# Four quarter loads of the input rows: issued together, or each when the one ahead has landed

## The chip, the cores and the metric

The kernel runs on one core of one Trainium2 chip. The time is device microseconds of that core for one execution, from the runtime's start of the program to its end; the profile's span (first to last instruction) is a little shorter. The engines are TensorE (PE in the rows; PEld is its weight load), VectorE (DVE), ScalarE (ACT), GpSimd (POOL) and SyncE (SP). A q behind an engine's name marks its queue, that is, instructions that only issue transfers. All inputs and outputs are in HBM; transfers from any engine move on the core's 16 DMA engines.

## The reference

One decoder step over 264 tokens (256 prompt rows, 8 decode rows) of width 1024, depth 1, all in float32. Cut to what matters here:

```python
def layer(x, ...):                    # x: 264 rows of 1024
    xn = rmsnorm(x, norm1)            # x * rsqrt(mean(x*x) + 1e-5) * norm1
    m, conv_new, ret_new = mixer(xn, ...)   # proj = xn @ w_in (1024 x 11264), short conv, retention
    h = x + m
    return h + moe_ffn(rmsnorm(h, norm2), ...)   # top 4 of 32 experts, clamped SwiGLU, 1024 wide
```

The first thing computed is therefore the sum of squares of each input row, the gain norm1, and the product of the rows with the first columns of w_in. The expert weights, 402 MB, are the bulk of all bytes.

## The kernel before

Every engine has its own instruction stream, and semaphores connect them. The mixer comes first, in an order of PE work that `mixer_order` writes out; weights come in 60 chunks of 1024 KB (`w_mixer`), which SP loads into a ring of 12 slots, each slot again as soon as its chunk was read. Then come routing and the experts in 16 pairs (`w_pairs`), whose weights SP loads in transfers of 2048 and 4096 KB, also slot by slot.

**The start, around the change.** The input rows are loaded turned (features along partitions) as `x_turned`, into `x_raw`: 8 groups of 128 features (k = 0 to 7) by 264 rows. `RAW_PARTS = 4` loads of two groups each (a quarter, 264 KB, `RAW_KS = 2`) stand at the head of ACT's stream (L915 to L917) and count the semaphores `raw_in[0..3]`. SP at the same time issues `par` (L636, 84 KB, the gains), the first two chunks of weights as 8 loads of 256 KB, one for each k (`load_first`, L634), tables (L623) and then whole chunks (L643).

- ACT: a dummy Sqrt (L923, it brings the table load with it), then for each quarter a wait for `raw_in[part]` and a Square of it into `x_squares` (L926, L927). Then the Sqrt of the sums (L929).
- DVE: for each k, after the wait for the quarter, `x_gained[k] = x_raw[k] * norm1` (L1246). Behind all eight of these, in the order of the stream, the squares are added up in four steps: L1248, L1250, L1252 and L1254, the last of which counts `x_summed`. Later the reciprocal (L1256) and the scaled tables.
- PE: `WARMING = 9` products of ones by ones (L1746), which nobody reads, then `project_first` (L1726): for k = 0 to 7 it waits for the weights of k and for `x_gained[k]` and makes four products into four banks (L1736). A float32 product appears as two passes in the trace. Behind k = 4 (`SUMS_BEHIND`) stands one product with ones (L1742), which adds the squares over partitions; it waits for `x_summed`. PE's stream is in order, so k = 5, 6 and 7 stand behind that wait. Then the second projection (L1722) and so on.

```python
for k in range(KD):                                  # PE, project_first
    pe.wait_ge(first_w[k], 16)
    pe.wait_ge(xg_ready, k + 1)
    ...
    if k == SUMS_BEHIND:
        pe.wait_ge(x_summed, 1)
        fills(pe.matmul(fill(pe, "x_sums")[:, 0:T], ones[:, :], x_squares[:, 0, :], start=True, stop=True), "x_sums")
```

Of the kernel before, what the change touches and what calls it, by code (L numbers as in the profile page):

```python
# [75 lines left out]
RAW_PARTS = 4  # L76
SUMS_BEHIND = 4
RAW_KS = KD // RAW_PARTS
WARMING = 9
WHOLE_CHUNKS = PAIR_CHUNKS - 2  # L80
SCRATCH = 2048
ARENA = 21672
# [288 lines left out]
def build(nc, a, o):  # L371
# [4 lines left out]
    with ctx:  # L376
# [202 lines left out]
        def read(eng, name):  # L579
            bank, n = plan[name]  # L580
            eng.wait_ge(filled[bank], n)
            return psum[bank]
# [37 lines left out]
        def _(sp):  # L620
            def load_tables(n):
                c = slice(TABLE_PARTS[n], TABLE_PARTS[n + 1])
                sp.dma_start(cst[:, c], a["tables"][:, c]).then_inc(cst_in[n], 16)  # L623

            mixer = [last for *_, last in mixer_parts()]
            assert len(mixer) == MIXER_CHUNKS

# [284 lines left out]

        @block.scalar
        def _(ac):
            for part in range(RAW_PARTS):  # L915
                ks_in = slice(RAW_KS * part, RAW_KS * (part + 1))
                ac.dma_start(x_raw[:, ks_in, :], a["x_turned"][:, ks_in, :]).then_inc(raw_in[part], 16)  # L917
            for primed in (xg_lo,):
                ac.sem_inc(primed, PRIMED)
            ac.sem_inc(quarter_squared, SQUARES)  # L920
# [3 lines left out]
            for part in range(RAW_PARTS):  # L924
                ks_in = slice(RAW_KS * part, RAW_KS * (part + 1))
                ac.wait_ge(raw_in[part], 16)  # L926
                ac.activation(x_squares[:, ks_in, :], x_raw[:, ks_in, :], ACT.Square).then_inc(x_squared, 1)  # L927
            bank = read(ac, "x_sums")
            empties(ac.activation(rinv[:, :], bank[:, 0:T], ACT.Sqrt, scale=1.0 / D, bias=stat[:, 15:16]), "x_sums")  # L929
# [269 lines left out]
        def _(v):  # L1199
# [71 lines left out]
            def rotate(event):  # L1271

                _, (name, g), j = event
                dst, cs, sn = (qT, cos, sin) if name == "q" else (kT, cosk, sink)
                if g == 0:
                    cs, sn = cos_r, sin_r
                lo, hi = ("proj", (name, g), j - 1), event
                x1, x2 = read(v, lo)[:, 0:T], read(v, hi)[:, 0:T]

                def times(i, x, table):  # L1280
                    if (name, g) == ("k", 0):
                        return v.scalar_tensor_tensor(rot[:, i, :], x, DK ** -0.5, table, ALU.mult, ALU.mult)
                    return v.tensor_tensor(rot[:, i, :], x, table, ALU.mult)  # L1283

                own(times(0, x1, cs))
                own(times(1, x2, sn))
                empties(times(2, x1, sn), lo)
                empties(times(3, x2, cs), hi)
                settle()
                was_read(v, lo)  # L1290
                was_read(v, hi)
                v.tensor_tensor(dst[:, j - 1, :], rot[:, 0, :], rot[:, 1, :], ALU.subtract).then_inc(qk_ready, 1)
                v.tensor_tensor(dst[:, j, :], rot[:, 2, :], rot[:, 3, :], ALU.add).then_inc(qk_ready, 1)
                qk[0] += 2
                v.wait_ge(qk_ready, qk[0])
# [397 lines left out]
        def _(pe):  # L1693
# [19 lines left out]
            def project(event):  # L1713

                _, name, j = event
                rhs, groups = {"wa": (aT, 1), "wb": (rT, 2)}.get(name[0], (x_gained if name == ("k", 0) else xnT, 1))
                n = chunks_of(name, groups)
                bank = fill(pe, event)
                for k in range(KD * groups):
                    if j == 0 and k % 4 == 0:  # L1720
                        chunk_ready(n + k // 4)
                    ins = pe.matmul(bank[:, 0:T], weight(n + k // 4, k % 4)[:, 128 * j:128 * (j + 1)], rhs[:, k, :],  # L1722
                                    start=k == 0, stop=k == KD * groups - 1)
                fills(ins, event)
# [19 lines left out]
            pe.wait_ge(const_set, 2)  # L1744
            for _ in range(WARMING):
                pe.matmul(psum[SUM_BANK][:, 0:128], ones[:, :], ones[:, :], start=True, stop=True)  # L1746
# [485 lines left out]
```

## Time and profile before

| | |
|---|---|
| median of 3 runs | 1411.05 us (1409.99 to 1411.69) |
| profiled execution, its time | 1411.89 us |
| its span | 1410.1 us |
| mean granted TensorE clock | 0.991 |
| PE, DVE, ACT, POOL busy | 96%, 27%, 18%, 7% of the span |
| bytes moved | 519.97 MB, mean 369 GB/s |

The profiled execution's time is 1.8 us more than its span, the part before the first and behind the last instruction, and 0.84 us more than the median. Engines' busy shares are averages over the whole span; the views below are of stretches.

### The profile page before, as it was taken

Reading aid. Unit: us, or ns where it says so; the run is one execution under the profiler, and the core shown is the slowest. Engines: PE = TensorE matmul, PEld = TensorE weight load, DVE = VectorE, ACT = ScalarE, POOL = GpSimd, SP = SyncE. Lnnn points to the kernel's source line nnn. Section 1 sums busy time; section 2 is a strip of 40 time slices with the busy share of each in tenths; the row PEclk is TensorE's granted clock in tenths of the full one; section 3 lists DMA queues with packets and bytes.
Section 4 is the critical chain, followed back from the end, with each engine's and each line's share of the span. In section 5 each row is a group of like instructions: output and inputs, shape, how many; then the busy total and the mean of one; then the engine's idle time right before and its main releaser. Section 6 shows DMA issues by size and latency. Waiting matters only on the chain.

```text
span 1410.1 us, 17559 instructions
## 1 busy us (share of the span) xinstructions
PE 1349.3 (96%) x7309; PEld 712.2 (51%) x7309; DVE 387.8 (27%) x722; ACT 251.0 (18%) x385; POOL 97.4 (7%) x169
## 2 busy tenths in 40 slices
PE   9999999999999999999998989989899899999997
PEld 8668678888887443343442423323333333333334
DVE  4235443642501431222221211112211122122223
ACT  1233343320000431111111111011110111101103
POOL 1122212210000210000000000000000000000000
PEclk9999999999999999999999999999999999999999
DMA  9888879874444699999999999999999999999997
GB/s 366 329 301 307 302 263 333 314 289 149 178 165 172 251 417 424 432 431 430 430 432 433 432 431 431 432 432 432 431 433 432 431 431 431 432 432 422 427 425 280
DMA packets 47173, 519.97 MB, mean 369 GB/s; under 512 B 5610, under 2 KB 6810, under 8 KB 25076
## 3 DMA queue, kind: packets, MB, share of 16 engines
q1 hardware_dynamic: 31952, 469.49, 79.3%
q0 software_dynamic: 12896, 45.70, 9.6%
q10 hardware_dynamic: 2276, 4.09, 0.8%
q8 instruction: 35, 0.57, 0.2%
q14 instruction: 14, 0.11, 0.0%
HBM read 497.63 MB, written 21.67 MB: 368 GB/s over the span
## 4 chain that ended last, share of the span: by engine, by line
PE 67%; DMA 27%; DVE 3%; SPq 2%; issue 1%; ACT 1%; POOL 0%; DVEq 0%; POOLq 0%; ACTq 0%
PE bank L2069 24%; PE bank L1722 19%; DMA ring<-in_w_pairs 13%; DMA arena<-in_w_pairs 11%; PE bank L1773 4%; PE bank L2024 4%; PE bank L2123 3%; PE bank L2010 3%; PE bank L1870 2%; DMA arena<-in_state_ret 2%; SPq L722 2%; PE bank L1736 1%; PE bank L2067 1%; PE bank L2020 1%; PE bank L2100 1%
## 5 line engine op out<-in xcount | busy, mean ns | idle before, releaser
L2069 PE MATMUL bank<-ring,arena 128*64 128x512 f32 x1536 | 348.8, 606 | 31.0 <-DMA ring<-in_w_pairs 31.0
L1722 PE MATMUL bank<-arena,ring 128*128 128x264 f32 x1472 | 331.5, 387 | 0.4 <-DVE arena L1283 0.4
L1722 PEld LDWEIGHTS bank<-arena,ring 128*128 128x128 f32 x1472 | 278.7, 190 | 51.0 <-issue 3.1
L2069 PEld LDWEIGHTS bank<-ring,arena 128*64 128x64 f32 x1536 | 109.5, 139 | 247.8 <-issue 215.7
L2123 PE MATMUL bank<-ring,arena 128*64 128x512 f32 x704 | 158.5, 595 | 3.1 <-DMA ring<-in_w_pairs 3.1
L2069 PE MATMUL bank<-arena 128*64 128x512 f32 x512 | 116.2, 602 | 9.1 <-DMA arena<-in_w_pairs 9.1
L1621 DVE TENSOR_SCALAR arena<-bank 128x512 f32<-128x512 f32 x32 | 22.1, 692 | 282.1 <-PE bank L2069 282.1
L2123 PEld LDWEIGHTS bank<-ring,arena 128*64 128x64 f32 x704 | 50.5, 137 | 92.6 <-issue 91.1
L2069 PEld LDWEIGHTS bank<-arena 128*64 128x64 f32 x512 | 36.4, 138 | 81.6 <-issue 81.4
L1644 DVE COPY arena<-bank 64x512 f32<-64x512 f32 x31 | 21.2, 683 | 177.0 <-PE bank L2123 177.0
L896 POOL CAST arena<-cst 128x128 bf16 x16 | 4.7, 293 | 883.2 <-PE bank L2107 818.2
L1611 DVE TENSOR_TENSOR hs<-hs,bank 128x256 f32<-128x256 f32 x15 | 6.3, 421 | 205.9 <-PE bank L2020 205.9
L1142 ACT ACTIVATE arena<-bank 128x264 f32<-128x264 f32 x16 | 6.3, 391 | 311.6 <-PE bank L2088 311.6
L2123 PE MATMUL bank<-arena 128*64 128x512 f32 x240 | 53.8, 594 | 5.2 <-DMA arena<-in_w_pairs 5.2
L1773 PE MATMUL bank<-ring,arena 128*128 128x512 f32 x128 | 56.6, 595 | 0.0
L2024 PE MATMUL bank<-arena 128*128 128x512 f32 x120 | 55.5, 605 | 0.0
L2010 PEld LDWEIGHTS bank<-arena 128*128 128x128 bf16 x768 | 47.6, 98 | 13.0 <-issue 13.0
L2010 PE MATMUL bank<-arena 128*128 128x128 bf16 x768 | 51.9, 219 | 0.0
L1154 ACT ACTIVATE arena<-bank 64x512 f32<-64x512 f32 x31 | 18.4, 593 | 155.8 <-PE bank L2123 155.8
L1614 DVE TENSOR_TENSOR hx<-hx,bank 128x512 f32<-128x512 f32 x60 | 41.2, 687 | 16.8 <-PE bank L2024 16.8
L937 ACT ACTIVATE arena<-arena 128x1024 f32<-128x1024 f32 x32 | 33.6, 1051 | 41.1 <-DMA arena<-in_state_ret 40.5
L1145 ACT ACTIVATE arena<-arena 128x512 f32<-128x512 f32 x32 | 20.2, 630 | 114.7 <-DVE arena L1621 114.5
(270 smaller groups left out, 1042.8 us busy)
## 6 DMA issues: line engine op xcount, KB each, us to landing
ring<-in_w_pairs SPq DMA_DIRECT2D x54, 4096.0 KB, 28.9
arena<-in_w_pairs SPq DMA_DIRECT2D x18, 4096.0 KB, 27.1
ring<-in_w_pairs SPq DMA_DIRECT2D x30, 2048.0 KB, 18.0
ring<-in_w_mixer SPq DMA_DIRECT2D x58, 1024.0 KB, 8.9
arena<-in_w_pairs SPq DMA_DIRECT2D x10, 2048.0 KB, 29.3
arena<-in_state_ret POOLq DMA_DIRECT2D x32, 512.0 KB, 8.0
out_ret_sample<-arena POOLq DMA_DIRECT2D x32, 512.0 KB, 5.7
arena<-v_decode POOLq DMA_DIRECT2D x32, 256.0 KB, 6.6
```

The source lines that it names most:

```text
L722: sp.dma_start(dst[:, D * f:D * (f + 1)], mine[:, D * f:D * (f + 1)])\
L937: ac.activation(S[n % 3], S[n % 3], ACT.Copy, scale=gamma(n // NS)).then_inc(S_scaled, 1)
L1614: v.tensor_tensor(hx[:, t, 512 * c:512 * (c + 1)], hx[:, t, 512 * c:512 * (c + 1)], psum[ADD_BANKS[i + 1]][:, :], ALU.add).then_inc(added, 1)
L1621: v.tensor_scalar(gcl, psum[2 * e][:, :], LIMIT, None, ALU.min).then_inc(g_clip, 1)
L1644: v.tensor_copy(ysb[SLOTS * e:SLOTS * (e + 1), 0:512], psum[Y_BANKS[e]][0:64, :]).then_inc(y_ready, 1)
L1722: ins = pe.matmul(bank[:, 0:T], weight(n + k // 4, k % 4)[:, 128 * j:128 * (j + 1)], rhs[:, k, :], start=k == 0, stop=k == KD * groups - 1)
L1773: ins = pe.matmul(bank[:, :], xnT[:, k, 128 * t:128 * (t + 1)], w, start=k == 0, stop=k == KD - 1)
L1870: ins = pe.matmul(bank[:, :], merged[:, k, 128 * t:128 * (t + 1)], weight(n + 2 * c + k // 4, k % 4), start=k == 0, stop=k == KD - 1)
L2010: pe.matmul(out, xp[:, t, part, 128 * k:128 * (k + 1)], P[:, 2 * t:2 * t + 2, :], start=t == 0 and part == 0, stop=False)
L2024: pe.matmul(psum[ADD_BANKS[i + 1]][:, :], pgT[:, 128 * t:128 * (t + 1)], ysb[:, 512 * c:512 * (c + 1)], start=True, stop=True).then_inc(co ...
L2069: ins = pe.matmul(out, xgT[:, k, 64 * e:64 * (e + 1)], held(n, 2 * D * (k % W1_KS) + c), start=False, stop=k == KD - 1)
L2123: ins = pe.matmul(psum[Y_BANKS[e]][64 * side:64 * (side + 1), :], lhs, held(n, D * (f % W2_FS) + 512 * side), start=False, stop=f == KD - 1)
```

## The change

ACT issues only the first quarter at its start. Each later quarter is issued from the loop over the squares: after the wait for the quarter ahead of it, before the Square of that quarter. On PE, eight warming products stand in place of nine. Nothing else differs.

```diff
-WARMING = 9
+WARMING = 8
...
         @block.scalar
         def _(ac):
-            for part in range(RAW_PARTS):
+            def load_raw(part):
                 ks_in = slice(RAW_KS * part, RAW_KS * (part + 1))
                 ac.dma_start(x_raw[:, ks_in, :], a["x_turned"][:, ks_in, :]).then_inc(raw_in[part], 16)
+
+            load_raw(0)
             for primed in (xg_lo,):
                 ac.sem_inc(primed, PRIMED)
             ac.sem_inc(quarter_squared, SQUARES)
...
             for part in range(RAW_PARTS):
                 ks_in = slice(RAW_KS * part, RAW_KS * (part + 1))
                 ac.wait_ge(raw_in[part], 16)
+                if part + 1 < RAW_PARTS:
+                    load_raw(part + 1)
                 ac.activation(x_squares[:, ks_in, :], x_raw[:, ks_in, :], ACT.Square).then_inc(x_squared, 1)
```

ACT's stream at the start of the program, before (`arena<-in_x_turned` are the loads of the quarters, L927 the Squares, `raw_in0` to `raw_in3` the semaphores of the four landings):

```order
L917 DMA arena<-in_x_turned 128x528 x4
L923 ACT_TABLE_LOAD
L923 ACTIVATE stat<-stat 128x1 [waits const_set]
L927 ACTIVATE arena<-arena 128x528 [waits raw_in0]
L927 ACTIVATE arena<-arena 128x528 [waits raw_in1]
L927 ACTIVATE arena<-arena 128x528 [waits raw_in2]
L927 ACTIVATE arena<-arena 128x528 [waits raw_in3]
L929 ACTIVATE arena<-bank,stat 128x264 [waits filled5]
```

The same place in the changed kernel (its line numbers are 4 higher behind the loads, L931 is the Square):

```order
L917 DMA arena<-in_x_turned 128x528
L925 ACT_TABLE_LOAD
L925 ACTIVATE stat<-stat 128x1 [waits const_set]
L917 DMA arena<-in_x_turned 128x528 [waits raw_in0]
L931 ACTIVATE arena<-arena 128x528
L917 DMA arena<-in_x_turned 128x528 [waits raw_in1]
L931 ACTIVATE arena<-arena 128x528
L917 DMA arena<-in_x_turned 128x528 [waits raw_in2]
L931 ACTIVATE arena<-arena 128x528
L931 ACTIVATE arena<-arena 128x528 [waits raw_in3]
L933 ACTIVATE arena<-bank,stat 128x264 [waits filled5]
```

Three of the four loads moved behind the dummy Sqrt, and each now stands behind the wait for the landing of the quarter ahead of it; the Squares themselves follow in the same order.

## Rows read from the trace of the kernel before

**Rows 1.** Waits of PE from 24 to 600 us: who for whom, total, times, longest.
```profile
PE bank L1852 <- DVE arena L1335: 1.0, 1, 1.0
PE bank L1980 <- DVE arena L1539: 0.5, 1, 0.5
```

**Rows 2.** Waits of PE from 600 us to the end.
```profile
PE bank L2069 <- DMA ring<-in_w_pairs: 31.0, 18, 2.7
```

**Rows 3.** Stretches: length, busy (count) by engine, granted clock, DMA share, GB/s.
```profile
440.00:450.00 10.00, 10.00 (x47) 8.54 (x46) 0.86 (x2) 0.00 (x0) 0.00 (x0) 1.00 0.00 0
...
490.00:500.00 10.00, 9.41 (x82) 6.49 (x83) 7.21 (x30) 5.10 (x9) 1.63 (x2) 1.00 0.97 414
```

**Rows 4.** A stretch of the expert stage, same columns.
```profile
700.00:900.00 200.00, 185.35 (x976) 69.21 (x972) 38.38 (x60) 23.46 (x32) 1.62 (x7) 0.98 1.00 432
```

**Rows 5.** Timeline of PE, start: start us, us, instructions [idle before <-releaser].
```profile
1.23 4.18 PE L1746 MATMUL bank<-ones 128*128 128x128 f32 x18 [1.23 <-POOL rg L793]
6.40 11.14 PE L1736 MATMUL bank<-arena,ring 128*128 128x264 f32 x40 [0.99 <-DMA ring<-in_w_mixer]
17.37 0.61 PE L1742 MATMUL bank<-arena,ones 128*128 128x264 f32 x2
```

**Rows 6.** Timeline of ACT, start.
```profile
0.74 1.88 ACTq L917 DMA_DIRECT2D arena<-in_x_turned  x4
2.79 1.28 ACT L923 ACT_TABLE_LOAD   x1 [2.79 <-issue]
...
9.99 0.64 ACT L927 ACTIVATE arena<-arena 128x528 f32<-128x528 f32 x1 [0.75 <-DMA arena<-in_x_turned]
```

**Rows 7.** Timeline of DVE, start.
```profile
3.98 0.62 DVE L1246 TENSOR_SCALAR arena<-arena,short 128x264 f32<-128x264 f32 x2 [2.01 <-DMA arena<-in_x_turned]
...
9.99 0.62 DVE L1246 TENSOR_SCALAR arena<-arena,short 128x264 f32<-128x264 f32 x2 [0.76 <-DMA arena<-in_x_turned]
...
12.63 0.43 DVE L1254 TENSOR_TENSOR arena<-arena 128x264 f32<-128x264 f32 x1
```

**Rows 8.** Passes of L1736 from 7.1 to 9.9 us: ns minimum/median/maximum.
```profile
L1736 PE MATMUL bank<-arena,ring x8: 647/647/809, 6.4 to 9.6; 128*128 128x264 f32 x8
```

**Rows 9.** Passes of L1736 from 11 to 17 us.
```profile
L1736 PE MATMUL bank<-arena,ring x29: 386/386/386, 10.7 to 16.9; 128*128 128x264 f32 x29
```

**Rows 10.** Timeline of SP, start.
```profile
1.22 4.26 SPq L634 DMA_DIRECT2D ring<-in_w_mixer  x8
```

**Rows 11.** Transfers issued before 13 us: KB each, median us from issue to landing.
```profile
ring<-in_w_mixer SPq DMA_DIRECT2D x8, 256.0 KB, 7.6
arena<-in_x_turned ACTq DMA_DIRECT2D x4, 264.0 KB, 6.2
cst<-in_tables SPq DMA_DIRECT2D x1, 528.0 KB, 8.5
```

**Rows 12.** Stretches at the start, columns as in rows 3.
```profile
0.00:5.00 5.00, 3.77 (x18) 3.80 (x18) 0.69 (x4) 2.02 (x3) 1.49 (x12) 1.00 0.60 163
5.00:10.00 5.00, 4.01 (x10) 2.97 (x10) 1.26 (x5) 1.30 (x3) 0.00 (x0) 1.00 1.03 371
10.00:15.00 5.00, 5.00 (x23) 4.21 (x22) 2.99 (x6) 0.63 (x1) 0.00 (x0) 1.00 1.04 420
```

**Rows 13.** DMA from 182 to 185.6 us: packets, MB, share by queue; ACT's load issued.
```profile
q1 hardware_dynamic: 194, 1.46, 96.9%
...
v_kept<-arena ACTq DMA_DIRECT2D x1, 512.0 KB, 8.5
```

**Rows 14.** Timeline of PE, 766 to 774 us.
```profile
772.01 2.83 PE L2069 MATMUL bank<-ring,arena 128*64 128x512 f32 x6 [2.73 <-DMA ring<-in_w_pairs]
```

**Rows 15.** Stretch behind that wait, columns as in rows 3.
```profile
772.00:776.00 4.00, 3.99 (x12) 1.41 (x14) 0.00 (x0) 0.00 (x0) 0.00 (x0) 0.62 1.03 442
```

**Rows 16.** Timeline of PE, 884 to 890 us.
```profile
888.60 1.94 PE L2069 MATMUL bank<-ring,arena 128*64 128x512 f32 x8 [2.71 <-DMA ring<-in_w_pairs]
```

**Rows 17.** Stretch around that wait, columns as in rows 3.
```profile
884.00:888.00 4.00, 1.89 (x10) 0.43 (x6) 0.00 (x0) 0.00 (x0) 0.00 (x0) 1.00 0.97 418
```

## The prediction

> **What bounds the kernel now.** I read first the waits of PE, by stretch. From 24 to 600 us PE waits for next to nothing: 1.0 and 0.5 us are its longest waits [rows 1]. From 600 us on it waits 31.0 us for expert weights in the ring alone [rows 2], and there the DMA engines move 432 GB/s at a share of 1.00 [rows 4]: that stage is bound by transfers. Then the stretches at the seam between the two. From 440 to 450 us nothing is moved at all, because no slot is free, and PE is busy throughout; from 490 us on 414 GB/s flow [rows 3]. So the stream that bounds the second half starts when PE frees slots. The reader is to see that no slack lies between start and end: PE late by d at 20 us frees slots d later, the stream starts and ends d later. A gain at the start carries over in the same way. So the question is when PE passes its start.
>
> The start itself, from three timelines. PE makes its warming products from 1.23 to 5.41 us, waits for the weights of k = 0 until 6.40, and reaches the product over the squares (L1742) at 17.37 [rows 5]. DVE begins the gains of the last quarter at 9.99 and the last sum of squares at 12.63; that takes 0.43, so `x_summed` is there at 13.06 [rows 7]. L1742 hence doesn't wait: the squares are 4.3 us early. That slack is what the change spends.
>
> **Loads of the first weights.** They are issued at 1.22 [rows 10] and used 5.2 us later [rows 5]. The four quarters are issued back to back from 0.74 [rows 6], so most of that time two queues share the engines. With one quarter in flight, the weights of k = 0 (256 KB against 264 KB of a quarter [rows 11]) have the engines nearly alone behind the first quarter. One load of 256 KB at the 371 GB/s of the second stretch [rows 12] is 0.7 us, so I let them land 1.3 to 1.8 us sooner, by 4.6 to 5.1.
>
> **The warming product.** Nine take 4.18 us [rows 5], one 0.46, so eight end near 4.95. PE can begin k = 0 at about 5.0 instead of 6.40. The product itself costs nothing on the path where it only filled a wait.
>
> **PE until L1742.** The 40 passes run at two paces. From 6.4 to 9.6 us eight start, 0.46 us apart [rows 8]; from 10.7 to 16.9 there are 29, 0.22 apart [rows 9]. The clock column reads 1.00 throughout, but the pace says 1.2 GHz up to about 10.4 us and 2.4 GHz behind it. From 5.0, 40 passes at 0.22 end at 13.9; with the change of pace at 10.4 as here, 12 passes are slow and 28 fast, and they end at 16.6. So PE is at L1742 at 13.9 to 16.6.
>
> **The later quarters, the term that decides.** A quarter's trip was from 0.74 to 3.98, 3.2 us, with only the 84 KB of gains ahead of it [rows 6, 7]. That is the lower bound for a trip made alone. The upper one is ACT's load of 512 KB at 182.02, with SP's queue full: 8.5 us, in the first 3.6 of which ACT's queue (q10) has no packet in the list while SP's takes 96.9% [rows 13]. So a newly issued load first waits behind what SP has put ahead, and then shares. How long depends on the size of SP's rows: 8 KB a partition there, 2 KB in the first weights.
> - Second and third quarter: SP's loads around them are those of 256 KB, so I stay near the lower bound, at 3.5 us. The second is issued at 3.95 (ACT is free: its table load moves ahead of the loads) and lands at 7.5, the third is issued at 7.6 and lands at 11.1. PE needs them for k = 2 and k = 4, after 16 and 32 passes: at 8.5 and 12.0 at the earliest. Both are in time.
> - Fourth quarter, issued at 11.15. By then SP has gone through its small loads. Ahead of its first load of 1024 KB stand 84 + 8 x 256 + 528 KB and three quarters, 3.5 MB. By 10 us 2.7 MB were moved, and 420 GB/s follow [rows 12]: the large load begins near 12.05, just before the fourth quarter's packets can. The lower bound is 3.2 us (14.4). The upper one is the 3.6 of waiting and half of the other 4.9 us of the 512 KB, 6.1 (17.2). I take 5.1, nearer to the upper, since the large load's rows are the size seen there; but a part of what stands ahead is still the table of 528 KB, with rows of half that size. It lands at 16.2, against 9.97 before.
> - From the fourth quarter to `x_summed` DVE takes 3.1 us (9.99 to 13.06) [rows 7]; that chain doesn't change. So `x_summed` comes at 19.3, and L1742 starts at 19.3 instead of 17.37: **+1.9 us**. PE stands idle 2.7 to 5.4 us before it.
>
> The Trainium skill has another price for a trip: DMA: Bandwidth & Descriptors, section "Anatomy of one DMA", gives some 2.0 us fixed and bytes at 436 GB/s. By that estimate a quarter takes 2.6 us, the fourth lands at 12.0, `x_summed` comes at 15.1, and the term would be about -2.3 us at the fast pace. No row here shows such a trip; the first quarter's is 3.2.
>
> **The clock behind that wait.** After 2.73 us of idle time PE ran slowly: the granted clock is 0.62 over 772 to 776 us, which loses 1.5 us [rows 14, 15]. After an idle time of 2.71 us at 885.9 it stayed 1.00 [rows 16, 17]. So a wait of this length sometimes costs the clock; mine is as long or longer. At the start nine passes at 0.44 instead of 0.22 cost 2.0 us before the pace doubled. I take **+2.0** (bounds 0 and 3).
>
> **What moves at no cost.** The Squares of the first three quarters begin 0.45 us later behind an issue; they aren't what DVE waits for, the fourth has no issue ahead of it. SP's and POOL's streams are untouched, and SP's order too; its chunks for the second projection have landed long before PE needs them. DVE's reciprocal and tables hang on L1742 and shift with PE. Nothing is cheaper downstream.
>
> **The sum.** +1.9 + 2.0 = +3.9 against the profiled execution (1411.89, span 1410.1). Its start stage lies anywhere within the spread of 1.7 us of the three runs, so I add 3.8 to the median: **1414.9 us**.
>
> **Rivals.**
> 1. Short trips. If each later trip is as long as the first one, 3.2, the quarters land at 7.15, 10.4 and 13.6, `x_summed` comes at 16.7, and L1742 starts 0.7 us earlier than before: 1410.4. For it: the first quarter shared with the rows of gains and did so. Against it: 528 KB of table and the large load are in front of the fourth. It decides where the fourth lands by 14.3. The Trainium skill's trip of 2.6 us would end here too, near 1408.8 by estimate. Chance 0.22, of which 0.03 are for a gain over 0.2%.
> 2. The quarter is late, the clock holds. As in rows 16 and 17: +1.9, 1413.0. Chance 0.15.
> 3. All three trips are long. At 5.1 each, quarters land at 9.1, 14.2 and 19.4, PE waits for k = 4 too, and L1742 starts at 22.5: +5.1 + 2.0, 1418.1. Chance 0.08.
> 4. The stage bound by transfers swallows the shift, because the stream would have begun then anyway: 1411.1. The empty stretch at 440 us speaks against it. Chance 0.05.
>
> **How the numbers follow.** My forecast has 0.50. 0.2% of the time, 2.8 us, is about what a measurement of this kernel can tell from no change. The forecast's own range is +2.2 to +6, and a fifth of it lies under 2.8. Slower: 0.40 of the forecast, 0.08 of rival 3, 0.04 of rival 2, in all 0.52. Within 0.2%: 0.10, 0.19, 0.11 and 0.05, in all 0.45. Faster: 0.03. The range goes from rival 1 (1410.0, with the runs' spread) to rival 3 (1418.0).
>
> **What would show it.** In the profile of the changed kernel: PE's first L1740 pass near 5.0; three loads on ACT's queue at 3.95, 7.6 and 11.2; DVE's gains of the last quarter from about 16.3; L1746 (the old L1742) at 19.3 with a wait for DVE ahead of it of over 2.5 us; passes behind it at 0.44 us for a few us; PE's waits between 24 and 600 us unchanged. The prediction is wrong if the last quarter's gains start before 14.5, or if the second half's stream doesn't begin as much later as L1746 does.

## The result, and the profile after

| | before | after |
|---|---|---|
| median | 1411.37 us (4 runs, 1409.99 to 1412.13) | 1425.76 us (4 runs, 1424.49 to 1426.49) |
| ratio, 95% interval | | 1.0095 [1.0081, 1.0110] |
| profiled execution, span | 1411.89, 1410.1 | 1425.51, 1423.6 |

The change costs 14.4 us of the median and 13.5 us of the span. I forecast slower by 3.8 and a range to 1418.0; the time lies far above it. The direction was right and the size wrong by a factor of nearly four.

ACT's timeline of the changed kernel, at the start (start us, us, instructions, idle before and its releaser), answers to [rows 6]:

```profile
0.74 0.42 ACTq L917 DMA_DIRECT2D arena<-in_x_turned  x1
1.33 1.28 ACT L925 ACT_TABLE_LOAD   x1 [1.33 <-PEq L2222]
...
3.81 0.35 ACTq L917 DMA_DIRECT2D arena<-in_x_turned  x1
4.21 0.64 ACT L931 ACTIVATE arena<-arena 128x528 f32<-128x528 f32 x1 [1.38 <-DMA arena<-in_x_turned]
10.96 0.33 ACTq L917 DMA_DIRECT2D arena<-in_x_turned  x1
11.34 0.64 ACT L931 ACTIVATE arena<-arena 128x528 f32<-128x528 f32 x1 [6.48 <-DMA arena<-in_x_turned]
18.22 0.34 ACTq L917 DMA_DIRECT2D arena<-in_x_turned  x1
18.60 0.64 ACT L931 ACTIVATE arena<-arena 128x528 f32<-128x528 f32 x1 [6.63 <-DMA arena<-in_x_turned]
25.66 0.64 ACT L931 ACTIVATE arena<-arena 128x528 f32<-128x528 f32 x1 [6.41 <-DMA arena<-in_x_turned]
```

The reader is to see three trips, one behind the other: 3.81 to 10.96, 10.96 to 18.22, 18.22 to 25.66, that is 7.15, 7.26 and 7.44 us. The last quarter is used at 25.66 in place of 9.99. DVE's timeline shows the same chain of sums behind it as [rows 7], 3.1 us long:

```profile
25.66 0.62 DVE L1250 TENSOR_SCALAR arena<-arena,short 128x264 f32<-128x264 f32 x2 [6.81 <-DMA arena<-in_x_turned]
...
28.29 0.43 DVE L1258 TENSOR_TENSOR arena<-arena 128x264 f32<-128x264 f32 x1
```

PE's timeline, start, against [rows 5]:

```profile
1.23 3.75 PE L1750 MATMUL bank<-ones 128*128 128x128 f32 x16 [1.23 <-POOL rg L793]
5.75 9.51 PE L1740 MATMUL bank<-arena,ring 128*128 128x264 f32 x32 [0.77 <-DMA ring<-in_w_mixer]
18.73 3.08 PE L1740 MATMUL bank<-arena,ring 128*128 128x264 f32 x8 [3.47 <-DVE arena L1250]
28.78 1.25 PE L1746 MATMUL bank<-arena,ones 128*128 128x264 f32 x2 [6.97 <-DVE arena L1258]
29.82 7.17 PE L1740 MATMUL bank<-arena,ring 128*128 128x264 f32 x24
36.83 8.40 PE L1726 MATMUL bank<-arena,ring 128*128 128x264 f32 x37
```

The first weights did come sooner, but less than forecast: PE begins k = 0 at 5.75 instead of 6.40. Then it waits 3.5 us for the third quarter at k = 4, and 7.0 us for the sums. The product over the squares starts at 28.78, 11.4 us later than before. That is the last quarter's 15.7 us less the 4.3 us by which the sums had been early. The second projection (L1722, now L1726) started at 23.16 before, behind the 24 passes of k = 5 to 7, as two more lines of PE's timeline of before show:

```profile
17.82 5.50 PE L1736 MATMUL bank<-arena,ring 128*128 128x264 f32 x24
23.16 14.40 PE L1722 MATMUL bank<-arena,ring 128*128 128x264 f32 x64
```

It starts at 36.83 now, 13.7 us later. The 2.3 us between the two are the clock. Two stretches behind the wait (columns as in rows 3) show it at half, 1.2 GHz, and back at 2.4:

```profile
28.70:33.20 4.50, 4.42 (x10) 3.49 (x11) 2.60 (x4) 0.48 (x1) 0.00 (x0) 0.50 1.02 424
33.20:37.00 3.80, 3.80 (x18) 3.25 (x18) 0.76 (x3) 0.00 (x0) 0.57 (x1) 1.00 1.01 418
```

The rest of the program is the old one, shifted. The stretch in which nothing is transferred [rows 3] now lies 14 us later, and the expert stage moves the same 432 GB/s [rows 4]:

```profile
454.00:464.00 10.00, 10.00 (x47) 8.54 (x46) 0.86 (x2) 0.00 (x0) 0.00 (x0) 1.00 0.00 0
504.00:514.00 10.00, 9.41 (x82) 6.41 (x83) 7.45 (x30) 5.04 (x9) 2.19 (x3) 1.00 0.98 415
...
700.00:900.00 200.00, 187.28 (x987) 70.75 (x985) 39.19 (x61) 25.28 (x35) 1.95 (x8) 0.98 1.00 432
```

SP's first expert loads of that stage show the shift to a tenth. The row before, and the row after:

```profile
452.54 0.80 SPq L733 DMA_DIRECT2D ring<-in_w_pairs  x2
```

```profile
465.98 1.15 SPq L733 DMA_DIRECT2D ring<-in_w_pairs  x2
```

13.4 us later, and the span is 13.5 longer.

How little of a newly issued quarter moves at first is seen in the DMA view of the changed kernel from 3.8 to 7.4 us, then from 10.9 to 14.3, the stretches behind ACT's issues at 3.81 and 10.96 (packets, MB, share by queue). One queue is listed in either, SP's; ACT's has no packet:

```profile
q1 hardware_dynamic: 557, 1.01, 91.1%
```

```profile
q1 hardware_dynamic: 292, 1.48, 104.2%
```

### The profile page after: what moved, and what is told of

It reads as the page before. It is cut to its first block, busy times and chain, and to the rows that moved or that the text cites. A ratio compares the mean times of both kernels' runs of the same rounds, so it can differ in the third digit from the quotient of the medians.

```text
span 1423.6 us, 17555 instructions
## 1 busy us (share of the span) xinstructions
PE 1356.3 (95%) x7307; PEld 714.0 (50%) x7307; DVE 387.7 (27%) x722; ACT 251.0 (18%) x385; POOL 97.4 (7%) x169
## 4 chain that ended last, share of the span: by engine, by line
PE 66%; DMA 28%; DVE 3%; SPq 2%; issue 1%; ACT 1%; POOL 0%; DVEq 0%; POOLq 0%; ACTq 0%
PE bank L2073 24%; PE bank L1726 19%; DMA ring<-in_w_pairs 13%; DMA arena<-in_w_pairs 11%; PE bank L1777 4%; PE bank L2028 4%; PE bank L2127 3%; PE bank L2014 3%; PE bank L1874 2%; DMA arena<-in_x_turned 2%; SPq L722 2%; DMA arena<-in_state_ret 2%; PE bank L2071 1%; PE bank L2024 1%; PE bank L2104 1%
## 5 line engine op out<-in xcount | busy, mean ns | idle before, releaser
L1726 PE MATMUL bank<-arena,ring 128*128 128x264 f32 x1472 | 331.5, 387 | 0.4 <-DVE arena L1287 0.4
L1726 PEld LDWEIGHTS bank<-arena,ring 128*128 128x128 f32 x1472 | 278.7, 190 | 51.0 <-issue 3.1
L1648 DVE COPY arena<-bank 64x512 f32<-64x512 f32 x31 | 21.2, 683 | 175.9 <-PE bank L2127 175.9
## 6 DMA issues: line engine op xcount, KB each, us to landing
ring<-in_w_pairs SPq DMA_DIRECT2D x30, 2048.0 KB, 18.3
```

Source lines behind the costliest of these rows:

```text
L1648: v.tensor_copy(ysb[SLOTS * e:SLOTS * (e + 1), 0:512], psum[Y_BANKS[e]][0:64, :]).then_inc(y_ready, 1)
```

## The experiments

All are compared with the kernel before on the same chip (medians 1410.25, 1411.49 and 1411.16 us in the three groups of runs). What decides is mostly the profile's start, since it resolves tenths and the shift was seen to carry to the end. The changed kernel wasn't run again beside them, so its time is compared with theirs by what each costs over the kernel before, 14.4 us for the change.

**Nine warming products in the changed kernel.**

```diff
-WARMING = 8
+WARMING = 9
```

> The changed kernel with nine warming products again. Theory (the chained trips of the quarters of 7.1 to 7.4 us cause all of the 14.4 us): PE's first pass of L1740 moves from 5.75 to at most 5.9, the product over the squares stays at 28.8 us (it waits for DVE), and the time stays 1425.8 within 1 us. Rival (the missing warming product keeps the clock low): the time falls by 2 us or more toward 1423.

1425.54 us (1423.66 to 1431.52), ratio 1.0108 [1.0074, 1.0142]. PE's first pass came at 5.99, the product over the squares at 29.18 behind a wait of 8.0 us for DVE. That is 15.3 us above the kernel before, against the change's 14.4, so nothing speaks for the warming product as a part of the loss.

**Fillers in PE's two waits.** 14 products of ones ahead of the wait at k = 4 and 36 ahead of the wait for the sums, in addition to the work of the kernel.

```diff
+                    for _ in range(14 if k == SUMS_BEHIND else 0):
+                        pe.matmul(psum[SUM_BANK][:, 0:128], ones[:, :], ones[:, :], start=True, stop=True)
                     pe.wait_ge(xg_ready, k + 1)
...
+                        for _ in range(36):
+                            pe.matmul(psum[SUM_BANK][:, 0:128], ones[:, :], ones[:, :], start=True, stop=True)
                         pe.wait_ge(x_summed, 1)
```

> The changed kernel with 14 more products of ones ahead of PE's wait at k = 4 and 36 ahead of its wait for the squares, which nobody reads, so PE idles little in the two waits. The landings don't change: the product over the squares stays at 28.8 us. If the idle waits cost the clock, the passes behind it stand 0.22 apart and not 0.44, the second projection starts at 34.5 to 35 in place of 36.8, and the time falls by 2 to 2.4 us to 1423.5. If the clock is no part of the loss, it stays 1425.8.

1424.58 us (1423.64 to 1425.56). PE's timeline:

```profile
21.67 8.20 PE L1748 MATMUL bank<-ones 128*128 128x128 f32 x72
30.05 0.71 PE L1750 MATMUL bank<-arena,ones 128*128 128x264 f32 x2 [0.17 <-DVE arena L1258]
30.60 5.50 PE L1742 MATMUL bank<-arena,ring 128*128 128x264 f32 x24
35.94 6.39 PE L1726 MATMUL bank<-arena,ring 128*128 128x264 f32 x28
```

The last quarter came 1.3 us later in this execution (26.92), so the product over the squares wasn't at 28.8. But from it to the second projection it is 5.9 us here and 8.05 in the changed kernel: the clock's term is 2.2 us, as the 2.3 above says. The stretch behind, 30.6 to 36.0, has a granted clock of 1.00. The time doesn't show it: it is 14.3 us above the kernel before where the change costs 14.4, and I had expected 2 to 2.4 less. In the profiled execution the late landing took back 1.3 us; for the other executions there is no profile that would tell. So the clock's term rests on profiles alone.

**The product over the squares last.**

```diff
-SUMS_BEHIND = 4
+SUMS_BEHIND = 7
```

> The changed kernel with the product over the squares behind k = 7 in place of k = 4, so k = 5 no longer stands behind the last quarter and the chain of four sums is beside k = 6 and 7. Theory (the last landing at 25.6 and the 3.1 us of DVE's sums behind it set the end of the first projection): k = 5 is made during the wait, k = 6 starts at 26.0, the second projection at 33 to 33.5 in place of 36.8, and the time falls by 3 to 4 us to 1422. If only the number of waits counted, it stays 1425.8.

1421.67 us (1420.79 to 1425.59), 11.4 above the kernel before where the change costs 14.4: 3.0 less. k = 5 moved into the wait, and k = 6 and 7 run beside DVE's sums; the second projection starts at 31.16, 5.7 earlier, more than I gave, since the clock had risen again (granted clock 0.50 from 23.0 to 24.0 us, 0.98 from 24.0 to 25.5). Of that, 1.1 us are lost later, where the second projection waits for a bank that DVE empties late. So the last landing sets the end, and what stands behind it in PE's order is paid on top.

**How long is a trip, and why.** Four kernels vary what SP does around it. First, SP waits behind every second of its eight small loads for the landing of a quarter, so that two of them at most stand ahead:

```diff
             for k in range(KD):
                 load_first(k)
+                if k % 2 == 1:
+                    sp.wait_ge(raw_in[k // 2], 16)
```

> The changed kernel, but SP waits for the landing of quarter k // 2 behind every second of its first eight weight loads, so at most two loads of 256 KB stand ahead of each later quarter and none of 528 or 1024 KB. Theory A (a later quarter waits behind what SP has handed over): trips shrink from 7.1 to 3.2 to 4 us, the last quarter lands at 13.5 to 16 us in place of 25.6, the product over the squares starts at 16.7 to 19.2 in place of 28.8, the time is 1412 to 1415.5. Theory B (a load that ACT issues behind a wait takes 7 us whatever SP does): last quarter at 25 us, time 1425 or more.

1418.19 us (1416.28 to 1420.78), ratio 1.0052 [1.0034, 1.0070]. ACT's timeline:

```profile
3.80 0.36 ACTq L919 DMA_DIRECT2D arena<-in_x_turned  x1
...
8.75 0.36 ACTq L919 DMA_DIRECT2D arena<-in_x_turned  x1
...
13.27 0.36 ACTq L919 DMA_DIRECT2D arena<-in_x_turned  x1
...
17.73 0.64 ACT L933 ACTIVATE arena<-arena 128x528 f32<-128x528 f32 x1 [3.41 <-DMA arena<-in_x_turned]
```

Trips of 4.95, 4.5 and 4.5 us: shorter, so theory B falls, but longer than theory A's 3.2 to 4. The last landing at 17.7 and a product over the squares at 20.85 are outside its numbers too, and so is the time.

Second, SP silent behind its first two small loads until the last quarter has landed:

```diff
                 load_first(k)
+                if k == 1:
+                    sp.wait_ge(raw_in[RAW_PARTS - 1], 16)
```

> The changed kernel, but SP issues the rest of its loads (behind the first two of 256 KB) only when the last quarter has landed, so the later quarters travel alone. Theory (a trip alone costs 3 us, beside two small loads 4.6, in SP's full stream 7.2): the three later trips take 2.8 to 3.3 us each and the last quarter lands at 12.3 to 13.8 us. If the trip were long because of ACT's wait and issue, it would be 4.5 us or more here too. The time says little, since the weights of k = 2 come after 16 us: it is 1415 to 1425.

One run, 1417.13 us. ACT's timeline:

```profile
3.75 0.35 ACTq L919 DMA_DIRECT2D arena<-in_x_turned  x1
...
6.73 0.33 ACTq L919 DMA_DIRECT2D arena<-in_x_turned  x1
...
9.27 0.34 ACTq L919 DMA_DIRECT2D arena<-in_x_turned  x1
...
11.98 0.64 ACT L933 ACTIVATE arena<-arena 128x528 f32<-128x528 f32 x1 [1.69 <-DMA arena<-in_x_turned]
```

Alone, a trip is 3.0, 2.5 and 2.7 us, two of them shorter than I gave, and the last quarter is used at 11.98, ahead of my 12.3. (The first of the three began while the end of SP's two small loads was still moving.) ACT's wait and issue are in these, so they aren't what makes it long. The two that were quite alone are near the 2.6 us that comes, by estimate, from the Trainium skill's sum (DMA: Bandwidth & Descriptors, "Anatomy of one DMA"). The section gives that sum for a transfer that GpSimd issues, and these are ACT's; beside SP's loads no trip came below 4.5 us.

Third, SP issues all eight small loads and nothing behind them until the last quarter has landed. No row of 8 KB is about:

```diff
             for k in range(KD):
                 load_first(k)
+            sp.wait_ge(raw_in[RAW_PARTS - 1], 16)
```

> The changed kernel, but SP stops behind its eight loads of 256 KB (rows of 2 KB) until the last quarter has landed. It tells whether the long trip needs SP's rows of 8 KB. Theory (a later quarter waits for what SP has handed over before it, whatever the size of its rows): quarter 1 is still late, at 10 to 11 us, though only rows of 2 KB are about; the weights are through by 11.5 us, so quarters 2 and 3 travel alone, 2.5 to 3 us each, and land at 13 to 14.5 and 15.7 to 17.3. Rival (as in my prediction, the wait grows with the size of the rows): quarter 1 lands by 8.

One run, 1414.40 us. ACT's timeline:

```profile
3.72 0.35 ACTq L918 DMA_DIRECT2D arena<-in_x_turned  x1
...
11.10 0.33 ACTq L918 DMA_DIRECT2D arena<-in_x_turned  x1
...
13.78 0.33 ACTq L918 DMA_DIRECT2D arena<-in_x_turned  x1
...
16.39 0.64 ACT L932 ACTIVATE arena<-arena 128x528 f32<-128x528 f32 x1 [1.58 <-DMA arena<-in_x_turned]
```

One trip of 7.4 us with rows of 2 KB alone around it, and two of 2.7 and 2.6 as soon as SP's loads are through. So the long trip is made by loads that SP has handed over, and it doesn't need rows of 8 KB. This is the experiment that refutes the step of my prediction.

Fourth, all three later quarters issued at once when the first has landed, one trip on the path:

```diff
-                if part + 1 < RAW_PARTS:
-                    load_raw(part + 1)
+                if part == 0:
+                    for late in range(1, RAW_PARTS):
+                        load_raw(late)
```

> Quarters 1 to 3 are all issued when the first has landed, so only one trip is on the path instead of three. Theory (each wait for a landing costs a trip of 7 us beside SP's full queue, the bytes cost little): the three land at 10.9, 11.7 and 12.5 us, the sums are ready near 15.6, the product over the squares starts at 16.3 to 17.3, and the time is that of the kernel before within 1 us (1409.5 to 1411.5). Rival (a quarter that lands after SP's loads have begun is late however it is issued): the last lands after 18 us and the time is 1414 or more.

1413.11 us (12 runs, 1411.68 to 1416.24), ratio 1.0006 [0.9997, 1.0016]. The quarters are used at 10.90, 12.26 and 14.02: the first at the foreseen time, the others 0.6 and 1.5 later than foreseen:

```profile
10.90 0.62 DVE L1251 TENSOR_SCALAR arena<-arena,short 128x264 f32<-128x264 f32 x2 [6.42 <-DMA arena<-in_x_turned]
12.26 0.62 DVE L1251 TENSOR_SCALAR arena<-arena,short 128x264 f32<-128x264 f32 x2 [0.73 <-DMA arena<-in_x_turned]
14.02 0.62 DVE L1251 TENSOR_SCALAR arena<-arena,short 128x264 f32<-128x264 f32 x2 [1.14 <-DMA arena<-in_x_turned]
```

PE waits 2.6 us at k = 2 and is at the product over the squares at 18.51, not by 17.3, and the time is 1.6 us above the kernel before by the medians, not within 1; the interval includes no difference. Still, with one wait in place of three almost the whole loss is gone, with the same bytes and the same issuing engine.

**Two quarters ahead.** 0 and 1 issued at the start, 2 behind the landing of 0, 3 behind that of 1.

```diff
             load_raw(0)
+            load_raw(1)
...
-                if part + 1 < RAW_PARTS:
-                    load_raw(part + 1)
+                if part + 2 < RAW_PARTS:
+                    load_raw(part + 2)
```

> Quarters 0 and 1 are issued at the start, 2 when 0 has landed, 3 when 1 has landed: two trips on the path instead of three, the second of them from about 6 us. Theory: quarter 2 lands near 10.9 to 11.5, quarter 3 near 13 to 13.8, the sums are ready near 16.5, the product over the squares starts at 16.5 to 17.5, the time is that of before within 1 us. If ACT's trip counts from the end of SP's backlog and not from its own issue, quarter 3 lands with quarter 2.

1412.52 us (11 runs, 1410.18 to 1414.52), ratio 1.0008 [0.9999, 1.0016]. The quarters are used at 11.15 and 14.43, the product over the squares starts at 17.55: the last quarter is 0.6 later than I gave, the rest as foreseen to 0.1 us (the time is 1.0 us above, by the medians). Here the trips were 7.0 and 7.6, and the second began at 6.82: it counts from its own issue.

**Looking for a version that beats both.** No waits, but order of need: the first quarter from ACT, the others from SP between its weights (here `load_raw` issues on SP; ACT keeps its own issue of part 0 alone).

```diff
             for k in range(KD):
                 load_first(k)
+                if k in (1, 3):
+                    load_raw((k + 1) // 2)
+                if k == 4:
+                    load_raw(3)
...
                 ac.wait_ge(raw_in[part], 16)
-                if part + 1 < RAW_PARTS:
-                    load_raw(part + 1)
```

> The first quarter from ACT at the start, the other three from SP without any wait, between its weight loads in the order in which PE needs them (w0, w1, x1, w2, w3, x2, w4, x3, w5 to w7), eight warming products. Theory (order of need without waits keeps the early weights and loses no trip): the weights of k = 0 land by 4.6 to 5.2 us, x1 near 6.5, x3 by 10.5, L1740 starts by 5.2, the product over the squares at 15 to 16.7, and the time is 0.5 to 2 us under the kernel before. Rival (the early start is worth nothing because the clock sets the pace until 10 us): the same time as before.

1409.91 us (12 runs, 1409.04 to 1415.40), ratio 0.9996 [0.9984, 1.0009]. L1746 (here the passes of k = 0) starts at 5.60 and the product over the squares at 16.84, behind a slow pace until 10.2 us. Both are later than I gave, and so are the quarters (used at 7.77, 10.04 and 12.24); a gain isn't shown. The same with ten warming products:

```diff
-WARMING = 8
+WARMING = 10
```

> The version with the later quarters on SP's queue in order of need, with ten warming products in place of eight, so no idle time is left ahead of the weights at 5.6 us. Theory: the clock has risen by 5 to 8.5 us, PE is at the product over the squares by 15 to 15.5 (the sums are ready at 15.3), the time is 1.5 to 3 us under the kernel before. Rival (the rise isn't brought forward): as with eight, 1409.9.

1410.14 us (11 runs, 1408.09 to 1411.55), ratio 0.9992 [0.9983, 1.0001]. PE's timeline has the product at 14.89 and the second projection at 20.67, 2.5 us ahead of the kernel before, and the span is 1407.8:

```profile
5.88 9.17 PE L1746 MATMUL bank<-arena,ring 128*128 128x264 f32 x40 [0.59 <-DMA ring<-in_w_mixer]
14.89 0.61 PE L1752 MATMUL bank<-arena,ones 128*128 128x264 f32 x2
```

But the kernel before with another number of warming products shows how little one profile says at this size. First eight, then eleven:

```diff
-WARMING = 9
+WARMING = 8
```

> The kernel before with eight warming products, the other half of the change alone. Theory (the product only fills a wait for the weights): L1736 starts at 6.4 as before, and the time is that of before within 0.1%. Rival (the longer idle stretch ahead of the weights puts the clock's rise off by some us): 1 to 2 us slower.

```diff
-WARMING = 9
+WARMING = 11
```

> The kernel before with eleven warming products, so PE idles at most 0.3 us ahead of the first weights and not 1.0. If the idle stretch is what keeps the pace slow until 10.4 us, the passes of L1736 stand 0.22 apart from 5 to 8 us on, the product over the squares starts at 15.3 to 16.5 in place of 17.37, and the time is 1 to 2 us shorter. If the pace rises after 10 us anyway, the time is the same.

With eight: 1411.62 us (12 runs, 1409.74 to 1417.89), ratio 1.0005 [0.9992, 1.0018]; with eleven 1410.34 us (12 runs, 1409.11 to 1417.49), ratio 0.9997 [0.9982, 1.0012]. PE's timeline with eight, then with eleven:

```profile
6.49 9.17 PE L1736 MATMUL bank<-arena,ring 128*128 128x264 f32 x40 [1.51 <-DMA ring<-in_w_mixer]
```

```profile
6.41 9.17 PE L1736 MATMUL bank<-arena,ring 128*128 128x264 f32 x40 [1.14 <-DMA ring<-in_w_mixer]
```

Both make the 40 passes in 9.17 us, at the fast pace from the first, where the profile of before took 11.14 [rows 5]; with eight the idle stretch ahead was longer (1.51 against 0.99), not shorter. So my idea that the idle stretch holds the clock down is not borne out, and 2 us at the start come and go between executions of such kernels. None of these four kernels (order of need with eight and with ten, the one before with eight and with eleven) is shown to be faster than the kernel before; order of need with ten comes nearest, its interval ends at 1.0001. The waits cost; the warming product is worth nothing that can be measured either way.

## Why the prediction was wrong, by its steps

| step | as predicted | measured |
|---|---|---|
| PE begins k = 0 | 5.0 us | 5.75 |
| trips of the three later quarters | 3.5, 3.5, 5.1 us | 7.15, 7.26, 7.44 |
| last quarter used | 16.2 | 25.66 |
| product over the squares | +1.9 | +11.4 |
| clock behind the wait | +2.0 | +2.3 |
| carried to the end | all | span +13.5 of 13.7 |
| median | +3.8 | +14.4 |

- **The step that failed** is "Second and third quarter: SP's loads around them are those of 256 KB, so I stay near the lower bound, at 3.5 us", with the reason given ahead of it, that the wait depends on the size of SP's rows. In the changed kernel, ACT's queue moves nothing in the 3.6 us behind its issue at 3.81, with rows of 2 KB in the other queue (the DMA view above), as at 182 us with rows of 8 KB [rows 13].

  [rows 13] had the right wait. I scaled it down by a factor that no row showed, and I read the first quarter's 3.2 us as a lower bound near which others would lie, while it was the trip of a load issued ahead of everything. The first wait then delays the issue of the next, so the error of 3.65, 3.76 and 2.34 us came in three times, 9.5 us of landing (with 0.3 us of issue gaps the other way).

  What stood in its place, by the trace of the changed kernel: 3.4 to 3.7 us until ACT's first packet, then 2.9 to 3.1 us in which both queues have packets (7.5 to 10.4 for the quarter issued at 3.81), then 0.5 to 0.8 us until it is used. The 3.5 us left room for neither the wait nor the sharing. With SP silent the first packet comes 0.95 us behind the issue and the packets take 1.2 to 1.6.
- The fourth quarter's term, worked out from bytes moved and rows, was off by 2.3 us of trip; its time of issue was off by 7.1. Its upper bound of 6.1 was too low as well: it halved the 4.9 us behind the wait with the bytes, and the three quarters took 3.5 to 3.9 us there. Its lower bound, 3.2, wasn't one either: alone it was 2.5 to 3.0.
- The weights of k = 0 were used at 5.75 and not at 5.0. That cost nothing, since PE waited at k = 4 anyway.
- Right: that nothing lies between start and end. SP's first loads of the expert stage are 13.4 us later, the span 13.5. In the twelve other profiles, too, the span moves as the start of the second projection does, within 0.8 us (1.0 with the product over the squares last). Rival 4 falls, with its chance of 0.05.
- Right: the chain of the sums (3.1 us), the slack of 4.3 us, and the clock's term, 2.3 against 2.0, which the profile with the fillers shows. The wait before it was 7.0 us and not 2.7 to 5.4; behind the 5.1 us of the kernel with two small loads ahead the granted clock was 0.50 too (20.8 to 25.0 us). Shorter waits go either way, as the prediction had it: behind 3.47 us at k = 4 it was 0.63 over 18.7 to 21.8 in the changed kernel, and 1.00 over 19.1 to 21.2 in the one with nine warming products. Rival 2 falls.
- Rival 3 was the mechanism as it happened, with trips at 5.1 in place of 7.3 and a chance of 0.08. Its upper bound stood in [rows 13] at 8.5 us for twice the bytes; had I used 6.1, the bound that I worked out from it, for all three, the sum would have been 3.95 + 18.3 + 3.1 = 25.4 for the product over the squares, and +8 + 2 in all, near 1421. The range stopped at 1418.0 and left out its own bound.
- Rival 1, short trips, is what happens when SP is silent (2.5 to 3.0 us); there is no such time at the start of this kernel.

What stays open is what a newly issued load waits for. The first packet comes 0.95 us behind the issue with SP silent, 1.5 to 1.6 beside two small loads, 3.4 to 3.7 in the changed kernel and 4.2 beside the eight small loads alone. For the first of the three trips the wait ends when about all that SP had handed over at its start has moved: 1.32 MB of 1.40 (the gains and five small loads) in the changed kernel, 0.60 of 0.61 with SP silent. For the second this doesn't hold: over 6 MB of SP's were handed over and not yet moved at 10.96, and 1.45 MB of them went ahead. Nor is it a fixed number of packets (some 560 in the first wait, most of 2 KB, and 280 in the second). No run separates a queue of requests from a longer path under load.

## What to carry to other kernels

A load that waits for another load's landing pays a whole trip, and the trip beside a busy stream is the one to price: here 7.3 us for 264 KB against 2.7 alone, and three in a row. Order loads by the order in which they are issued, not by waits for landings; where a wait is wanted, let all that follows hang on one. And if a bound has been worked out from a row, every term of that kind goes to it in the range, above all where terms follow one another in a chain.

## What the runs showed that I had not expected

- A load issued into the other queue moves nothing for some 3.5 us while SP's stream runs, with rows of 2 KB as of 8 KB, though its own 264 KB would take 0.7 us at 371 GB/s.
- PE's pace at the start rose at 10.4 us in the profile of before, and was high from the first real pass in two kernels that differ from it by one or two warming products only. That is 2 us of 1411 that no change of the kernel explains, about the spread of the medians.
